# Gate and up products of steps 8 and 9 of each feed-forward layer as seven block products, in a two-layer hybrid attention kernel

## The reference, cut to what matters

```python
SEQ, D_MODEL, D_FF, DEPTH = 256, 1024, 2816, 2

def _swiglu(x, w_gate, w_up, w_down):
    return (jax.nn.silu(x @ w_gate) * (x @ w_up)) @ w_down

for l in range(DEPTH):
    x = x + 0.5 * _swiglu(_rmsnorm(x, ffn1_norm[l]), ffn1_w_gate[l], ffn1_w_up[l], ffn1_w_down[l])
    ...   # projections, three attention branches, gates, w_out
    x = x + 0.5 * _swiglu(_rmsnorm(x, ffn2_norm[l]), ffn2_w_gate[l], ffn2_w_up[l], ffn2_w_down[l])
```

## Time and profile before

| | |
|---|---|
| median of 3 runs | 1159.79 us |
| the profiled execution | 1159.99 us, of which the span of the trace is 1158.2 us |
| PE busy | 1148.3 us (99%) |
| DVE busy | 935.0 us (81%) |
| ACT busy | 581.5 us (50%) |
| DMA queue of the weights | 55.2% of 16 engines |

### The profile page before, as it was taken

How to read it: one execution, slowest core, us unless ns; L and a number is a source line. 1 busy time by engine, 2 the same in 40 slices (tenths; PEclk the granted TensorE clock), 3 DMA queues, 4 the chain that set the end, 5 groups by cost and what they waited for, 6 DMA issues and landing times.

```text
span 1158.2 us, 16246 instructions
## 1 busy us (share of the span) xinstructions
PE 1148.3 (99%) x5525; PEld 940.3 (81%) x5525; DVE 935.0 (81%) x1734; ACT 581.5 (50%) x757; POOL 73.5 (6%) x133
## 2 busy tenths in 40 slices
PE   9999999999999999999999999999999999999997
PEld 6888888887777888888888888888877788888886
DVE  6877887878977688778887887877898696888877
ACT  6444345456764464344454444454678635434433
POOL 2000000061000000000000000002510000000000
PEclk9999999999999999999999999999999999999999
DMA  8566555796325555655556556557943345655570
GB/s 289 189 214 216 179 187 163 238 252 199 135 74 182 182 161 202 217 192 183 195 177 202 180 178 218 182 183 216 281 155 108 144 142 182 219 181 168 197 236 37
DMA packets 151042, 215.21 MB, mean 186 GB/s; under 512 B 9184, under 2 KB 110160, under 8 KB 150992
## 3 DMA queue, kind: packets, MB, share of 16 engines
q1 hardware_dynamic: 148256, 209.64, 55.2%
q0 software_dynamic: 2048, 4.20, 1.6%
q10 hardware_dynamic: 688, 0.71, 0.2%
HBM read 209.28 MB, written 1.05 MB: 182 GB/s over the span
## 4 chain that ended last, share of the span: by engine, by line
PE 96%; DMA 2%; DVE 1%; issue 0%; SPq 0%; ACT 0%; POOLq 0%; POOL 0%; DVEq 0%
PE ps L1393 30%; PE ps L1395 29%; PE ps L1394 29%; PE ps L1607 2%; PE ps L1663 1%; PE ps L1635 1%; PE ps L1443 1%; DMA raw<-in_w_in_dram 1%; PE ps L1412 1%; DMA x<-in_x_dram 1%; DVE wlo L547 0%; PE ps L1694 0%; PE ps L1654 0%; SPq L508 0%; PE ps L1578 0%
## 5 line engine op out<-in xcount | busy, mean ns | idle before, releaser
L547 DVE TENSOR_TENSOR wlo<-raw,whi 128x2048 fp32r<-128x2048 f32 (+1 forms) x195 | 433.7, 2242 | 79.8 <-ACT whi L1138 57.7
L1138 ACT ACTIVATE whi<-raw 128x2048 fp32r<-128x2048 f32 (+1 forms) x195 | 366.1, 1879 | 257.6 <-PE ps L1395 251.7
L1393 PE MATMUL ps<-whi,ht_hi 128*128 128x512 f32 (+1 forms) x1192 | 465.5, 391 | 0.6 <-DVE wlo L547 0.6
L1395 PE MATMUL ps<-whi,ht_lo 128*128 128x512 f32 (+1 forms) x1192 | 460.8, 387 | 0.0
L1394 PE MATMUL ps<-wlo,ht_hi 128*128 128x512 f32 (+1 forms) x1192 | 460.3, 386 | 0.0
L1395 PEld LDWEIGHTS ps<-whi,ht_lo 128*128 128x128 f32 x1192 | 223.9, 188 | 46.0
L1393 PEld LDWEIGHTS ps<-whi,ht_hi 128*128 128x128 f32 x1192 | 224.0, 188 | 45.6 <-ACT whi L1138 1.1
L1394 PEld LDWEIGHTS ps<-wlo,ht_hi 128*128 128x128 f32 x1192 | 224.1, 188 | 43.7
L609 DVE STREAM_TRANSPOSE scr<-scr 32x128 f32<-32x128 f32 x688 | 208.4, 303 | 10.3
L1393 PE MATMUL ps<-whi,at_hi 128*128 128x512 f32 x304 | 118.5, 390 | 0.0
L1394 PE MATMUL ps<-wlo,at_hi 128*128 128x512 f32 x304 | 118.3, 389 | 0.0
(11 more groups left out here) (179 smaller groups left out, 787.4 us busy)
## 6 DMA issues: line engine op xcount, KB each, us to landing
raw<-in_ffn_w_down_dram SPq DMA_DIRECT2D x88, 512.0 KB, 4.8
raw<-in_w_in_dram SPq DMA_DIRECT2D x88, 512.0 KB, 4.6
raw<-in_ffn_w_gate_dram SPq DMA_DIRECT2D x85, 512.0 KB, 4.0
raw<-in_ffn_w_up_dram SPq DMA_DIRECT2D x85, 512.0 KB, 5.0
raw<-in_w_out_dram SPq DMA_DIRECT2D x16, 512.0 KB, 4.5
raw<-in_w_branch_c_dram SPq DMA_DIRECT2D x8, 512.0 KB, 4.2
qk<-gates POOLq DMA_DIRECT2D x32, 64.0 KB, 2.9
gates<-prob POOLq DMA_DIRECT2D x32, 64.0 KB, 6.3
```

What stands on the lines that cost most here:

```text
L547: nc.vector.tensor_tensor(wlo[:, n, 0:w], raw[:, n, 0:w], whi[:, n, 0:w].bitcast(F32), ALU.subtract).then_inc(lo_done, 1)
L1138: nc.scalar.activation(whi[:, n, 0:w], raw[:, n, 0:w], ACT.Copy).then_inc(hi_done, 1)
L1393: nc.tensor.matmul(o, xh, wh, start=start, stop=False)
L1395: return nc.tensor.matmul(o, xl, wh, start=False, stop=stop)
```

## The change

`PAIR` = 8: steps 8 and 9 no longer have gate-up slabs of their own. Their gate and up products are one product of 256 tokens x 1024 by 1024 x 1024 columns (512 gate, 512 up), cut in 2 x 2 blocks: token halves, halves of the contracted width, and gate against up. Seven block products of 128 x 512 by 512 x 512 give it (`gate_up_pair`), each of 12 matmuls; before there were eight of 12. For that DVE and ACT make four sums of blocks of the input (`side_sums`, ten instructions of 128 x 512, then rounding and rest) and four sums of blocks of the weights (`block_sum`, 128 x 2048 each, T1 to T4, then `sum_round` on ACT and `sum_rest` on DVE). The four weight blocks are loaded whole beside the ring (eight DMAs of 512 KB, in steps 2 to 4), and three of them a second time through the ring (slabs 23 and 24 with half a block each, then 25 and 26). Sums of the results are made by `pair_sums` and `pair_products`.

This extra work stands in DVE's order in steps 1 to 7, each time between the conversion of slab 3i+4 and `act_rest(i)`: `side_sums` in step 1, four `side_rest` in step 2, weight sums in steps 3 to 5 (one, two, one), their rests in steps 5 to 7 (one, two, one).

Steps 0 to 7 are turned by 16 instructions as before, now into `act_blocks`, where each writes 128 adjacent elements. Steps 8 to 10 are turned by two 128-partition instructions each, and 16 DMAs of 16 KB each carry the blocks to their partitions: eleven from POOL, five from ACT. The loops of DVE, ACT and SP are written out. `silu(i+1)` now waits for the products of step i, not for `act_rest(i)`. PE's order at the end is `gate_up_pair`, `gate_up(10)`, `down(7)`, `down(8)`, `down(9)`, `down(10)`.

```diff
+PAIR = NSTEP - 3
+PAIR_SLAB = 3 * PAIR - 1
+OUT_SLAB = PAIR_SLAB + 6
+SUMS = ["T1", "T3", "T2", "T4"]
...
+        BY_ACT = [(3, 0), (3, 1), (3, 2), (3, 3), (2, 3)]
+        BY_POOL = [(a, q) for a in range(4) for q in range(4) if (a, q) not in BY_ACT]
...
+        def cross_act(eng, l, f, i, blocks, done):
+            eng.wait_ge(act_turned, (l * 2 + f) * NSTEP + i)
+            apart(eng)
+            for a, q in blocks:
+                blocks_in, blocks_out = act_set(i)
+                eng.dma_start(blocks_out[32 * q:32 * q + 32, P * a:P * a + P],
+                              blocks_in[32 * a:32 * a + 32, P * q:P * q + P]).then_inc(done[n_set(i)], 16)
...
             def turn_product(l, f, i):
...
-                for a in range(0, P, 32):
-                    for q in range(0, P, 32):
-                        ins = nc.vector.transpose(dst[q:q + 32, :, :, a:a + 32], src[a:a + 32, :, :, q:q + 32])
+                dve.wait_ge(act_done, (l * 2 + f) * (2 * NSTEP) + (PAIR * 2 + 4 if i == PAIR else i * 2 + 2))
+                if direct(i):
+                    src = act.rearrange("p t (j c) -> p t j c", j=2)
+                    dst = act_set(0)[1].rearrange("p (a j t c) -> p a t j c", a=4, j=2, t=NT)
+                    for a in range(4):
+                        for q in range(0, P, 32):
+                            ins = nc.vector.transpose(dst[q:q + 32, a], src[32 * a:32 * a + 32, :, :, q:q + 32])
+                else:
+                    src = act
+                    if PAIR <= i <= PAIR + 1:
+                        src = act_2[:, :, FSTEP * (i - PAIR):FSTEP * (i - PAIR) + FSTEP]
+                    dst = act_set(i)[0].rearrange("p (q j t c) -> p t q j c", q=4, j=2, t=NT)
+                    for t in range(NT):
+                        ins = nc.vector.transpose(dst[:, t], src[:, t, :].rearrange("p (j q c) -> p q j c", j=2, q=4))
                 ins.then_inc(act_turned, 1)
 
...
+            def side_sums(l, f):
...
+                dve.wait_ge(hth, (l * 3 + 2 * f) * KD + KD)
...
+                s1, s2, s3, s4 = side_raw
+                for o, a, b, op in ((s1, h21, h22, ALU.add), (s3, h11, h21, ALU.subtract), (s1, s1, l21, ALU.add),
+                                    (s3, s3, l11, ALU.add), (s1, s1, l22, ALU.add), (s3, s3, l21, ALU.subtract),
+                                    (s2, s1, h11, ALU.subtract), (s2, s2, l11, ALU.subtract),
+                                    (s4, h12, s2, ALU.subtract), (s4, s4, l12, ALU.add)):
+                    if done[0]:
+                        dve.wait_ge(side_sum, r * 10 + done[0])
+                    nc.vector.tensor_tensor(o, a, b, op).then_inc(side_sum, 1)
+                    done[0] += 1
+            def side_rest(l, f, m):
+                dve.wait_ge(side_h, (l * 2 + f) * 4 + m + 1)
+                nc.vector.tensor_tensor(side_lo[m], side_raw[m], side_hi[m].bitcast(F32), ALU.subtract).then_inc(side_l, 1)
...
+            def block_sum(l, f, m):
...
+                b11, b12, b22, b21 = (sum_raw[n][:, :] for n in SUMS)
...
+                    dve.wait_ge(part_in[n], (r + 1) * 32)
+                if m:
+                    dve.wait_ge(sum_done, r * 4 + m)
+                nc.vector.tensor_tensor(o, a, b, ALU.subtract).then_inc(sum_done, 1)
+            def sum_rest(l, f, m):
+                dve.wait_ge(sum_h, (l * 2 + f) * 4 + m + 1)
+                n = SUMS[m]
+                nc.vector.tensor_tensor(sum_lo[n][:, :], sum_raw[n][:, :], sum_hi[n][:, :].bitcast(F32), ALU.subtract)\
+                    .then_inc(sum_l, 1)
...
+            def pair_sums(l, f):
...
+                dve.wait_ge(pair_ps, r * 4 + 2)
+                nc.vector.tensor_tensor(v57, ps[:, 0, :], m5_out, ALU.add).then_inc(pair_sum, 1)
+                dve.wait_ge(pair_ps, r * 4 + 3)
+                nc.vector.tensor_tensor(u2, ps[:, 3, :], m1_out, ALU.add).then_inc(pair_sum, 1)
+                dve.wait_ge(pair_sum, r * 5 + 2)
+                nc.vector.tensor_tensor(up_1, v57, u2, ALU.add).then_inc(pair_sum, 1)
...
+            def pair_products(l, f):
...
+                wait_used(dve, l, s0 + PAIR_SLAB + 3)
+                nc.vector.tensor_tensor(up_0, ps[:, 2, :], u2, ALU.add).then_inc(pair_sum, 1)
+                dve.wait_ge(pair_sum, r * 5 + 4)
+                dve.wait_ge(silu_done, r * (2 * NSTEP) + PAIR * 2 + 2)
+                nc.vector.scalar_tensor_tensor(act_2[:, 0, :], up_0, rstd[:, 0:1], sg_2[:, 0, :], ALU.mult,
+                                               ALU.mult).then_inc(act_done, 2)
+                dve.wait_ge(pair_ps, r * 4 + 4)
+                nc.vector.tensor_tensor(gate_1, ps[:, 0, :], u2, ALU.add).then_inc(pair_sum, 1)
+                dve.wait_ge(silu_done, r * (2 * NSTEP) + PAIR * 2 + 4)
+                nc.vector.scalar_tensor_tensor(act_2[:, 1, :], up_1, rstd[:, 1:2], sg_2[:, 1, :], ALU.mult,
+                                               ALU.mult).then_inc(act_done, 2)
...
-                with dve.Fori(1, last - 1) as i:
-                    convert(l, (i, s0 + 2))
+                for i in range(1, PAIR):
+                    w = SLAB // 2 if i == PAIR - 1 else SLAB
+                    convert(l, s0 + 3 * i + 2, w)
                     products(l, f, i)
                     turn_product(l, f, i)
-                    convert(l, (i, s0 + 3))
-                    convert(l, (i, s0 + 4))
+                    convert(l, s0 + 3 * i + 3, w)
+                    convert(l, s0 + 3 * i + 4)
+                    if i == 1:
+                        side_sums(l, f)
+                    if i == 2:
+                        for m in range(4):
+                            side_rest(l, f, m)
+                    for m in {3: (0,), 4: (1, 2), 5: (3,)}.get(i, ()):
+                        block_sum(l, f, m)
+                    for m in {5: (0,), 6: (1, 2), 7: (3,)}.get(i, ()):
+                        sum_rest(l, f, m)
                     act_rest(l, f, i)
-                convert(l, s0 + 3 * last - 1)
-                products(l, f, last - 1)
-                turn_product(l, f, last - 1)
-                convert(l, s0 + 3 * last)
-                act_rest(l, f, last - 1)
...
+                convert(l, s0 + PAIR_SLAB + 3)
+                convert(l, s0 + PAIR_SLAB + 4)
+                pair_sums(l, f)
+                convert(l, s0 + PAIR_SLAB + 5)
+                pair_products(l, f)
+                turn_product(l, f, PAIR)
+                turn_product(l, f, PAIR + 1)
+                convert(l, s0 + OUT_SLAB)
+                convert(l, s0 + OUT_SLAB + 1)
                 products(l, f, last)
                 turn_product(l, f, last)
-                convert(l, s0 + 3 * last + 2)
+                act_rest(l, f, PAIR)
+                convert(l, s0 + OUT_SLAB + 2)
+                act_rest(l, f, PAIR + 1)
+                convert(l, s0 + OUT_SLAB + 3)
                 act_rest(l, f, last)
...
+            def ffn(l, f):
+                norm(l * 3 + 2 * f)
+                for i in range(PAIR, NSTEP):
+                    cross_act(pool, l, f, i, BY_POOL, act_crossed_rest)
...
+                for i in range(1, PAIR):
+                    w = SLAB // 2 if i == PAIR - 1 else SLAB
+                    convert(l, s0 + 3 * i + 2, w)
                     silu(l, f, i, False)
-                    convert(l, (i, s0 + 3))
-                    convert(l, (i, s0 + 4))
+                    convert(l, s0 + 3 * i + 3, w)
+                    convert(l, s0 + 3 * i + 4)
...
+                wait_used(eng, l, s0 + PAIR_SLAB + 1)
+                nc.scalar.activation(m1_out, ps[:, 1, :], ACT.Copy).then_inc(pair_out, 1)
+                convert(l, s0 + PAIR_SLAB + 4)
+                eng.wait_ge(pair_ps, (l * 2 + f) * 4 + 1)
+                nc.scalar.activation(m5_out, ps[:, 2, :], ACT.Copy).then_inc(pair_out, 1)
+                convert(l, s0 + PAIR_SLAB + 5)
+                wait_used(eng, l, s0 + PAIR_SLAB + 2)
+                pair_silu(l, f, 0, ps[:, 1, :])
+                convert(l, s0 + OUT_SLAB)
+                eng.wait_ge(pair_sum, (l * 2 + f) * 5 + 5)
+                pair_silu(l, f, 1, gate_1)
+                cross_act(eng, l, f, PAIR, BY_ACT, act_crossed)
+                cross_act(eng, l, f, PAIR + 1, BY_ACT, act_crossed)
+                convert(l, s0 + OUT_SLAB + 1)
                 silu(l, f, last, False)
-                convert(l, s0 + 3 * last + 2)
+                act_round(l, f, PAIR)
+                convert(l, s0 + OUT_SLAB + 2)
+                cross_act(eng, l, f, last, BY_ACT, act_crossed)
...
+            def gate_up_pair(l, f):
...
+                pe.wait_ge(act_done, r * (2 * NSTEP) + PAIR * 2)
+                for h in range(2):
+                    product(1, quadrant(halves, 0, 0), from_ring(s0 + PAIR_SLAB + h, 2), True, 2 * h)\
+                        .then_inc(slab_used, 1)
+                pe.wait_ge(side_l, r * 4 + 4)
+                product(2, s1, from_sums("T1"), True).then_inc(pair_ps, 1)
```

(17 more changed lines are left out.)

189 lines of the change are left out of this document (153 added, 36 removed).

## The result

The changed kernel takes 1194.76 us (median of four runs, 1192.62 to 1196.19) against 1159.80 for the kernel before on the same chip: a ratio of 1.030 (95% interval 1.028 to 1.032), slower by 35.0 us. The forecast was 1178.8 us, range 1162 to 1190: the direction was right, the size was not, and the time lies above the range. The profiled execution took 1193.44 us, of which the span is 1191.7; against the earlier trace rows the span is 33.5 us longer.

A forecast was written before the change was run, and what follows sets the result against it. PE was taken to bound the kernel, busy 1148.3 of 1158.2 us. Four blocks, each 7.46 us of stall less 2.72 saved, gave +19.0 on the profiled 1159.99, or 1179.0; forecast 1178.8 us, range 1162 to 1190.

The forecast's parts named there:

- The ledger of DVE: Steps 1 to 7 of each block: DVE's work summed step by step against PE's due times; PE waits 7.5 us.
- Its side sums: Step 1 on DVE: ten chained 128 x 512 instructions, each waiting for the one before, cost 7.2 us.
- A sign that failed: DVE in steps 1 to 7: no idle time from the first products to the conversion of slab 24.
- the sum ended a wait where PE starts again: PE's waits for DVE in steps 1 to 7: counted at their own length only, 7.46 us per block.
- the crossings at zero: End of each block: DMAs carrying turned blocks across partitions cost PE nothing, last set ready at 26.3, wanted at 27.2.
- rival (b): End of each block: crossing DMAs land late, at 6.3 us, adding 2.5 us per block, 1188.8 us; 13 in 100.
- nothing behind the last matmul: Program end: the sum held only PE's stalls and savings in four blocks, with no term for the end.
- Slab 24: Step 7, before the pair: half slab converted at 111.9, PE due at 110.4, so PE waits 1.5 us.
- Rival (a): DVE's turns of steps 0 to 7: writing 128 adjacent elements cuts a turn to 3.3 us, 1154.9 us; 12 in 100.
- Rival (c): DVE's extra work in steps 1 to 7 costs less, stalls of 2.5 to 4 us, 1158 to 1165 us; 12 in 100.
- ACT's roundings, the loads and the written-out loops: Whole block: roundings fit ACT's pauses, loads cost zero or 1 us per block at worst, written-out loops zero.

The follow-up runs named there:

- The spread kernel: Changed kernel with the same DVE instructions in another order, sums and remainders spread over steps 1 to 7, slab 24 before the turn of step 7: 1169.09 us (1.0079).

## Why the prediction was right in direction and short by 16 us

- **The ledger of DVE held.** Expected per block 3.3, 0.1, 1.3, 1.3 and, at slab 24, 1.5, 7.5 in all; measured 3.3, 0.2, 1.15, 1.15 and 1.23, 7.1. Its side sums took 7.1 us against 7.2. The spread kernel, which is the same ledger in another order, came within 1 us of its forecast of 1168. The Trainium skill (VectorE: DVE Perf Modes, "The DRAIN you can't avoid") says, from copies, that a chain of waits costs nothing. That does not hold for these sums: ten of them take 7.1 us, not 6.0.
- **A sign that failed: DVE did pause.** "DVE should show no idle time from the first products to slab 24", but in steps 3 and 4 it waits for silu, 1.2 (1.0 to 1.6) and 0.8 us. Silu follows PE's matmuls, and these lost 1.75 us at 1.2 GHz in block 2. With that, silu of step 3 begins at 32.64 + 3.3 + 1.75 on the ledger's scale and the products 0.51 later, at 38.2, while the ledger has DVE free at 37.0: 1.2 us, as measured. The pause is longest in the block where most was lost (2.9 us lost, 1.6 us idle). By this working the low clock made PE later for the next waits, which alone would have shortened them, and DVE's pauses made them as long again. That the 7.1 came so near to 7.5 is in part luck.
- **Step that failed: the sum ended a wait where PE starts again.** It priced a wait of PE at its own length. Behind the 3.3 us PE loses 1.6 to 2.9 us more at 1.2 GHz, 8.0 in all, for which the sum had no term; behind each of the others some 0.13, 2.6 in all. These are 10.6 us of the 14.4 by which the profiled run passed its forecast, 1179.0. No row of the kernel before shows PE resume from such a wait (its longest is 1.3 us); the text neither named it nor bounded it, and it should have been a range of its own.
- **Step that failed: the crossings at zero.** They were found hidden "by 0.9 us" for the last set alone, in front of down(10), and there PE indeed does not wait. It waits in front of down(8), for the first set, which the text did not reckon: 3.5 us over four blocks. In block 1 ACT issues ten DMAs one behind another, in front of its next conversion, its silu and its rounding:

```profile
165.24 3.76 ACTq L534 DMA_DIRECT2D act_blocks<-act_blocks  x5
169.12 3.10 ACTq L534 DMA_DIRECT2D T_raw<-T_raw  x5
172.32 1.92 ACT L1327 ACTIVATE whi<-raw 128x2048 fp32r<-128x2048 f32 x1 [8.86 <-issue]
...
1164.75 0.63 ACT L1377 ACTIVATE bt_hi<-act_blocks 128x512 fp32r<-128x512 f32 x1 [3.81 <-DMA act_blocks<-act_blocks]
```

An issue on ACT takes 0.61 us and not 0.4, which was one plain output DMA of the earlier trace rows. The last row is block 4, where ACT waits for the landing itself, up to 5.8 us behind the issue: rival (b) in small, and at the first set. POOL's issue (0.49, priced 0.58) was no problem.

- **Step that failed: nothing behind the last matmul.** "The sum" ended with PE. POOL's drain grew from 2.0 to 6.9 us and adds 2.1.
- Together: -1.5 (28.3 us of waits in steps 1 to 7 where 29.8 were reckoned) + 3.5 + 10.6 + 2.1 = 14.7, for a difference of 14.4. The median lies another 1.3 us above the profiled run; no trace shows where.
- **Slab 24** was put at 1.5 for DVE being late. The size was near by luck, the reason incomplete: with DVE in time it waits 1.27 all the same, and moving one instruction takes it away.
- **Rival (a)** is out: L700 is 303 ns and 5.05 us for 16, whatever it writes. **Rival (c)** is out, since the waits took 28.3 us of the 29.8 reckoned. That ACT's roundings, the loads and the written-out loops cost next to nothing was right: without the sums, and with slab 24 put right, what is left are down(8) and the drain.

## What to carry to other kernels

An engine that runs just ahead of PE has a budget per step, not per block: with the same instructions the kernel was 35 us slower in lumps and 9 spread out, and in these runs only waits of 2 us and more were followed by a lower clock. Before an idle engine is given work, look at which instructions of its neighbour run beside it: POOL's two-operand work left DVE's turns at 5.05 us, and two of DVE's subtractions took 8.92 us beside it for 4.49. Price a wait of PE with what the matmuls behind it lose, reckon the first use of a DMA and not only the last, and end the sum with the program, not with PE.

## What the runs showed of the hardware

- Waits of PE of 0.6 to 1.8 us left the clock at 2.4 GHz in 77 of 77 places; one of two waits of 2.0 us, 13 of 16 of 2.8 to 3.4 us, and all seven of 3.9 to 6.3 us were followed by matmuls at 1.2 GHz (0.43 us apart where they have 512 columns).
- A 128 x 2048 subtraction in float32 takes 4.8 us on POOL and 2.29 on DVE; if both run, one waits for the other (8.92 us for two of DVE's where 4.49 is usual). A turn in 32 x 128 pieces is untouched (5.05 us).
- Crossing DMAs of 16 KB follow one another in the issuing queue by 0.49 us on POOL, 0.64 on ACT and 0.63 on SP.
- POOL's closing drain is 2.0 to 10.0 us, and not in the order of the number of its DMAs (2.0 with 64, 10.0 with 163, 6.9 with 196).
- Ten chained 128 x 512 additions and subtractions on DVE, each waiting for the one before, take 7.1 us, 0.72 from start to start; four such subtractions without a wait between them start 0.60 apart.
